# Score products of two heads issued in turn in the short layers of a two-block transformer kernel

## What is computed

```python
def second_block(x, norm_g, w_in, w_out, diff_lam, diff_subln_g, final_norm_g):
    for layer in range(DEPTH):                       # DEPTH = 2
        h = _rmsnorm(x, norm_g[layer])
        proj = jnp.einsum('bsd,de->bse', h, w_in[layer])          # 2048 -> 8 parts of 256
        if layer % 2 == 0:
            oa = _dilated_mixture(_rope(_heads(qa), pos), _rope(_heads(ka), pos), _heads(va))
            ob = _moba(_rope(_heads(qb), pos), _rope(_heads(kb), pos), _heads(vb))
            y = concat(_merge(oa) * silu(ga), _merge(ob) * silu(gb))
        else:
            oc = _diff_attention(...)                # 4 heads, two score maps of 32 features each
            od = _stick_breaking(...)                # 4 heads of 64 features
            y = concat(_merge(oc) * silu(gc), _merge(od) * silu(gd))
        x = x + jnp.einsum('bse,ed->bsd', y, w_out[layer])
    return _rmsnorm(x, final_norm_g)
```

## Time and profile before

| | before |
|---|---|
| executions | 2729.01, 2729.70, 2726.66 us; median 2729.01 |
| profiled execution | span 2726.9 us from its first to its last instruction; no other time is listed for it |
| PE busy | 2696.2 us (99%) |
| DVE busy | 1694.4 us (62%) |
| ACT busy | 1343.5 us (49%) |
| PE waits by the list of waits, whole program | longest kinds 4.8, 4.8, 2.7, 1.4 and 1.3 us |
| layer 4, column slots 812 on | from about 2470 us |
| layer 5, column slots 852 on | from about 2605 us |

### The profile page before, as it was taken

One profiled execution on the slowest core, in us unless ns is written; L12 is line 12 of the kernel. 1 busy time (PEld: TensorE's weight loads), 2 busy tenths in 40 slices (PEclk: granted clock), 3 DMA queues, 4 the chain that ended last, 5 costly groups with the idle time before them and its releaser, 6 DMA issues.

```text
span 2726.9 us, 32209 instructions
## 1 busy us (share of the span) xinstructions
PE 2696.2 (99%) x12944; PEld 2241.6 (82%) x12944; DVE 1694.4 (62%) x2476; ACT 1343.5 (49%) x1952; POOL 63.2 (2%) x85
## 2 busy tenths in 40 slices
PE   9999999999999999999999999999999999999998
PEld 8778888888888888888888888888888888887877
DVE  5677675566666666545645555666666664466666
ACT  6645545464444444434545545644444443355565
POOL 0000000000000000000100000000000000000002
PEclk9999999999999999999999999999999999999999
DMA  7765647656666666656655435566666665565543
GB/s 231 136 139 140 127 122 135 206 186 200 198 194 194 193 193 193 193 193 204 213 172 155 115 110 176 187 193 193 194 193 194 193 195 193 193 202 165 164 137 132
DMA packets 213494, 480.54 MB, mean 176 GB/s; under 512 B 15584, under 2 KB 16480, under 8 KB 212704
## 3 DMA queue, kind: packets, MB, share of 16 engines
q1 hardware_dynamic: 210848, 467.27, 58.9%
q0 software_dynamic: 2352, 11.17, 1.1%
q10 hardware_dynamic: 144, 0.05, 0.0%
HBM read 476.32 MB, written 2.10 MB: 175 GB/s over the span
## 4 chain that ended last, share of the span: by engine, by line
PE 89%; DVE 5%; ACT 3%; issue 1%; DMA 1%; POOL 0%; SPq 0%; ACTq 0%; POOLq 0%
PE PS L1124 19%; PE PS L1126 19%; PE PS L1125 19%; PE PS L1171 8%; PE PS L1173 8%; PE PS L1172 8%; DVE WL L2192 2%; DVE WORK L2359 1%; ACT WH L1664 1%; PE PS L1386 1%; PE PS L1522 1%; PE PS L1099 1%; PE PS L1491 0%; DVE XL L2192 0%; DMA RAW<-in_ffn_w_down 0%
## 5 line engine op out<-in xcount | busy, mean ns | idle before, releaser
L2192 DVE TENSOR_TENSOR WL<-RAW,WH 128x1024 fp32r<-128x1024 f32 x826 | 1011.3, 1226 | 806.1 <-ACT WH L1664 803.6
L1664 ACT ACTIVATE WH<-RAW 128x1024 fp32r<-128x1024 f32 x830 | 875.3, 1056 | 918.8 <-PE PS L1126 609.3
L1124 PE MATMUL PS<-WH,UTH 128*128 128x512 f32 x2396 | 952.4, 397 | 5.0 <-DVE WL L2192 4.8
L1126 PE MATMUL PS<-WH,UTL 128*128 128x512 f32 x2396 | 935.5, 390 | 0.0
L1125 PE MATMUL PS<-WL,UTH 128*128 128x512 f32 x2396 | 934.7, 390 | 0.0
L1124 PEld LDWEIGHTS PS<-WH,UTH 128*128 128x128 f32 x2396 | 450.8, 188 | 102.1 <-DVE WL L2192 5.6
L1126 PEld LDWEIGHTS PS<-WH,UTL 128*128 128x128 f32 x2396 | 450.5, 188 | 96.4
L1125 PEld LDWEIGHTS PS<-WL,UTH 128*128 128x128 f32 x2396 | 451.2, 188 | 88.7
L1171 PE MATMUL PS<-WH,HTH 128*128 128x512 f32 x656 | 255.2, 389 | 0.0
L1172 PE MATMUL PS<-WL,HTH 128*128 128x512 f32 x656 | 255.2, 389 | 0.0
L1173 PE MATMUL PS<-WH,HTL 128*128 128x512 f32 x656 | 255.2, 389 | 0.0
(11 more groups left out here) (426 smaller groups left out, 2176.1 us busy)
## 6 DMA issues: line engine op xcount, KB each, us to landing
RAW<-in_ffn_w_gu SPq DMA_DIRECT2D x352, 512.0 KB, 4.5
RAW<-in_ffn_w_down SPq DMA_DIRECT2D x176, 512.0 KB, 4.4
RAW<-in_ab_w_in SPq DMA_DIRECT2D x128, 512.0 KB, 4.8
RAW<-in_nsa_w_in SPq DMA_DIRECT2D x80, 512.0 KB, 3.7
RAW<-in_w_in SPq DMA_DIRECT2D x64, 512.0 KB, 4.2
RAW<-in_ab_w_out SPq DMA_DIRECT2D x32, 512.0 KB, 4.3
RAW<-in_nsa_w_out SPq DMA_DIRECT2D x32, 512.0 KB, 4.2
RAW<-in_w_out SPq DMA_DIRECT2D x16, 512.0 KB, 4.4
```

The costliest lines, as they stand in the source:

```text
L1124: e.matmul(o, lh, wh[:, j], start=k + j == 0, stop=False)
L1126: x = e.matmul(o, ll, wh[:, j], start=False, stop=k + j == NKT - 1)
L1664: e.activation(wh, raw, ACTF.Copy).then_inc(*a_hi.inc(s))
L2192: e.tensor_tensor(wl, raw, wh.bitcast(F32), ALU.subtract).then_inc(*v_lo.inc(s))
```

## The change

Three steps of PE now make the scores of two heads in one go. They take two banks, and their matmuls alternate between the heads, which lie in different rows of the array: `pl_s(br, i)` for par 0 and 1, `df_s(pair, i)` for heads 2 pair and 2 pair + 1, `st_z(pair)` likewise. The parts that DVE and ACT had under the same names become steps of their own (`pl_x`, `df_x`, `st_x`), one a head: the first head's in the slot of the product, the second's one slot later. What follows (`pl_t`, `df_a`, `st_l`) is now placed from these. No instruction is added or removed on any engine; only order and banks differ.

```diff
+    def plain_scores(br, i):
+        yield from need(("feat", 4, 2 * br))
+        yield from pause(1 + 2 * i)
+        put("pl_s", br, i)
+        put("pl_x", br, 0, i)
+        yield
+        put("pl_x", br, 1, i)
+
     def plain(br, par, i):
-        yield from need(("feat", 4, 2 * br))
-        yield from pause(1 + 2 * par + i)
-        put("pl_s", br, par, i)
-        yield from pause(2)
+        yield from o.behind(2, ("pl_x", br, par, i))
         put("pl_t", br, par, i)
...
+    def diff_scores(pair, i):
+        yield from need(("feat", 5, 0))
+        yield from pause(1 + 4 * pair + 2 * i)
+        put("df_s", pair, i)
+        put("df_x", 2 * pair, i)
+        yield
+        put("df_x", 2 * pair + 1, i)
+
     def diff(h, i):
-        yield from need(("feat", 5, 0))
-        yield from pause(1 + 2 * h)
-        put("df_s", h, i)
-        yield from pause(2)
+        yield from o.behind(2, ("df_x", h, i))
         put("df_a", h, i)
...
+    def stick_scores(pair):
+        yield from need(("feat", 5, 2))
+        yield from pause(1 + 2 * pair)
+        put("st_z", pair)
+        put("st_x", 2 * pair)
+        yield
+        put("st_x", 2 * pair + 1)
+
     def stick(h):
-        yield from need(("feat", 5, 2))
-        yield from pause(1 + h)
-        put("st_z", h)
-        yield from pause(4 - h + h // 2)
+        yield from o.behind(4 - h + h // 2, ("st_x", h))
         put("st_l", h)
...
             @step
-            def pl_s(br, par, i):
-                P, T, s, nk = plain_of(br, par, i)
-                b = take("pl_s", br, par, i)
+            def pl_s(br, i):
+                nk = 128 * (i + 1)
+                b = [take("pl_s", br, par, i) for par in range(2)]
                 on.wait_ge(*a_b2.of("feat", 4, 2 * br, 2))
                 for j in range(2):
-                    q, k = qk_of(4, 2 * br, par + 2 * j)
-                    x = e.matmul(b[:, nk * j:nk * j + nk], q[:, 128 * i:128 * i + 128], k[:, 0:nk], start=True, stop=True)
-                x.then_inc(*p_b2.inc("pl_s", br, par, i))
+                    for par in range(2):
+                        q, k = qk_of(4, 2 * br, par + 2 * j)
+                        x = e.matmul(b[par][:, nk * j:nk * j + nk], q[:, 128 * i:128 * i + 128], k[:, 0:nk],
+                                     start=True, stop=True)
+                        if j == 1:
+                            x.then_inc(*p_b2.inc("pl_s", br, par, i))
```

More of the change, by code:

```diff
@@ L730, in write_order @@
     mixer(4, sink2[4], setup(4, 0, True), setup(4, 2, True),
-          *[plain(br, par, i) for br in range(2) for par in range(2) for i in range(2)],
+          *[plain_scores(br, i) for br in range(2) for i in range(2)],
+          *[plain(br, par, i) for br in range(2) for i in range(2) for par in range(2)],
           *[close(4, 2 * br + 1, *[[("pl_o", br, par, i) for par in range(2)] for i in range(2)])
@@ L738, in write_order @@
     mixer(5, sink2[5], setup(5, 0, True), setup(5, 2, False),
-          *[diff(h, i) for h in range(4) for i in range(2)], *[stick(h) for h in range(4)],
+          *[diff_scores(pair, i) for pair in range(2) for i in range(2)],
+          *[diff(h, i) for h in range(4) for i in range(2)],
+          *[stick_scores(pair) for pair in range(2)], *[stick(h) for h in range(4)],
           close(5, 1), close_diff(), close(5, 3),
@@ L1574, in df_s @@
             @step
-            def df_s(h, i):
-                P, T, s, nk = diff_of(h, i)
-                b = take("df_s", h, i)
+            def df_s(pair, i):
+                nk = 128 * (i + 1)
+                heads = (2 * pair, 2 * pair + 1)
+                b = {h: take("df_s", h, i) for h in heads}
                 on.wait_ge(*a_b2.of("feat", 5, 0, 2))
                 for j in range(2):
-                    q, k = qk_of(5, 0, h, j)
-                    x = e.matmul(b[:, nk * j:nk * j + nk], q[:, 128 * i:128 * i + 128], k[:, 0:nk], start=True, stop=True)
-                x.then_inc(*p_b2.inc("df_s", h, i))
+                    for h in heads:
+                        q, k = qk_of(5, 0, h, j)
+                        x = e.matmul(b[h][:, nk * j:nk * j + nk], q[:, 128 * i:128 * i + 128], k[:, 0:nk],
+                                     start=True, stop=True)
+                        if j == 1:
+                            x.then_inc(*p_b2.inc("df_s", h, i))
             @step
@@ L1604, in st_z @@
             @step
-            def st_z(h):
-                q, k = qk_of(5, 2, h)
-                b = take("st_z", h)
+            def st_z(pair):
+                heads = (2 * pair, 2 * pair + 1)
+                b = {h: take("st_z", h) for h in heads}
+                f = {h: tuple(qk_of(5, 2, h)) for h in heads}
                 on.wait_ge(*a_b2.of("feat", 5, 2, 2))
-                e.matmul(b[:, 0:256], k[:, 0:128], q, start=True, stop=True)
-                x = e.matmul(b[:, 256:384], k[:, 128:256], q[:, 128:256], start=True, stop=True)
-                x.then_inc(*p_b2.inc("st_z", h))
+                for h in heads:
+                    q, k = f[h]
+                    e.matmul(b[h][:, 0:256], k[:, 0:128], q, start=True, stop=True)
+                for h in heads:
+                    q, k = f[h]
+                    x = e.matmul(b[h][:, 256:384], k[:, 128:256], q[:, 128:256], start=True, stop=True)
+                    x.then_inc(*p_b2.inc("st_z", h))
             @step
@@ L2081, in pl_s, with pl_x @@
             @step
-            def pl_s(br, par, i):
+            def pl_x(br, par, i):
                 P, T, s, nk = plain_of(br, par, i)
@@ L2113, in df_s, with df_x @@
             @step
-            def df_s(h, i):
+            def df_x(h, i):
                 P, T, s, nk = diff_of(h, i)
@@ L2140, in st_z, with st_x @@
             @step
-            def st_z(h):
+            def st_x(h):
                 Zs, L = stick_of(h)
```

## The result

The changed kernel took 2738.39 us (median of 5 executions, 2737.49 to 2741.32) against 2728.99 us before (5 executions): 9.4 us longer. The ratio is 1.0038, 95% interval 1.0027 to 1.0049. I had forecast 2735.0, 6.0 us longer. The sign was right; the growth was half as large again as forecast.

What follows compares the result with a forecast made beforehand. PE, 99% busy, was taken as the bound, with the DVE and ACT chain slower where every slot has a link. 0.6 + 3.9 + 1.6 = 6.1 us gave 2735.1, say 2735.0; range 2728 to 2739, leaving out rival 4.

Steps and rivals of the forecast that it cites:

- PE's saving: Score steps of two heads side by side save 8.9 us of PE: layer 4 4.2, df_s 2.6, st_z 2.1.
- The chain: DVE and ACT's links delivering WH and WL, slower than PE's slot: +0.6 us in layer 4, +3.9 in layer 5.
- layer 4 at +0.6: Copies of pl_t now ahead of a prep lengthen the chain by 0.3 us a half; PE's saved 4.2 us return as waits.
- The term of +3.9 us: Layer 5: a link in each slot 856 to 863 delays the last scaling, so slot 868 starts 3.9 us later.
- The clock: One fall of PE's granted clock to 0.50 after the 3.3 us wait before the second st_z: +1.6 us.
- The signs: Wrong if slot 868 comes no later than 2662.80 + 1, layer 4 waits exceed 3 us, or growth lies in layer 4.
- Rival 1: PE waits for the chain but its clock does not fall: +4.5 us, 2733.5; chance 0.27.
- Rival 2: The two heads' products run one after another, mostly hidden by the chain: +1.1 us, 2734.6 to 2736.2; chance 0.13.
- Rival 3: PE's lead entering layer 5 covers the chain, last wait about 1 us without a fall: about 0, 2729; chance 0.12.
- Rival 4: Saved PE time reaches the end, if links cost under about 3.2 us: -8.9 us, 2720.1, half realised 2724.5; chance 0.08.

Runs made afterwards that it cites:

- even_later: Changed kernel with both softmaxes of a pair in their product's slot, and st_l, st_m, st_a, st_w in their slots from before; 2719.7 us, ratio 0.9968.
- changed_again: The changed kernel run once more without alteration, with a second profile; 2736.2 us, ratio 1.0032.
- serial: The changed kernel with the products of its joint steps issued one head after the other, not in turn; 2738.9 us, ratio 1.0035.
- keep_busy: The changed kernel with 8 to 13 products of zeros ahead of the four places where PE waited 1.8 to 2.9 us; 2733.3 us, ratio 1.0017.
- rhythm_only: The changed kernel with products again one head at a time, each in the slot of its softmax; softmaxes stay in the changed slots; 2731.1 us, ratio 1.0010.
- layer4_only: Layer 4 as in the changed kernel, layer 5 as before; 2732.5 us, ratio 1.0012.
- busy_single_z: As keep_busy, but st_z products one head at a time and the zeros for slot 863 moved to slot 864; 2736.6 us, ratio 1.0033.

## Why the prediction was right or wrong

**PE's saving: right.** 8.9 us of PE time, of which row groups running side by side was the unproven part. The records show it: eight in 0.72 us. In even_later, where nothing stands against it, the two layers are 4.5 + 3.6 = 8.1 us shorter. It is the Trainium skill's rule that small matmuls in different row groups run at once ("TensorE: Matmul & The Clock Gate", "Part 3: Packing small matmuls — row/col tiling"), and the traces now agree with it for row groups too.

**The chain: right, to a few tenths.** I had priced layer 4 at +0.6; with the clock held it was +0.7 (no run here separates its two halves). I had added up 33.0 us from the first to the last scaling of layer 5. The changed kernel's first is the mark at 2625.99; its seventh and last (timeline of DVE):

```profile
2652.76 0.69 DVE L2755 SCALAR_TENSOR_TENSOR WORK<-PS,BIG 128x512 f32<-128x512 f32 x1 [0.25 <-PE PS L1604]
2658.86 0.68 DVE L2755 SCALAR_TENSOR_TENSOR BIG<-PS,BIG 128x512 f32<-128x512 f32 x1
```

2658.86 - 2625.99 = 32.9. The last link, with passes of `st_z` in it, is 6.1 us, where 4.74 and the 1.15 and 0.3 that I had put there make 6.2. The term of +3.9 us measured +3.7 with the clock held. Together the chain costs 4.4 us where I had 4.5.

**The clock: the step that failed.** The prediction says "I add one fall, +1.6 us" and "A fall after an earlier wait costs nothing, since PE then meets the chain again." The first is wrong in number. I priced only the wait of 3.3 us, although show a stretch at 0.50 behind a wait of 2.36, and although I had myself forecast four more waits of about 2 us. The two profiles of the changed kernel have six and three stretches. The second sentence is wrong wherever the chain starts from PE again. In layer 4 the next meeting place lies behind `feat` and the score products of the second half, which PE itself must make first, so a stretch behind slot 822 is paid nearly in full (+2.2 or +2.3 instead of +0.7, for 1.7 us of lost work); the wait in slot 829 is 2.0 us with that stretch (changed_again) and without it (serial). In layer 5 it depends: in changed_again a stretch from 2646.4 on made the products of slot 862 late, and the scaling behind them waited for PE (timeline of DVE in changed_again):

```profile
2652.82 0.69 DVE L2755 SCALAR_TENSOR_TENSOR WORK<-PS,BIG 128x512 f32<-128x512 f32 x1 [1.54 <-PE PS L1604]
```

In the changed kernel's first profile, with its stretch at 2642, that wait was 0.25 us, and the stretch was mostly hidden by a shorter wait at the next bank, 0.6 us in slot 861 where changed_again waited 2.1. The term of +1.6 us measured 9.4 - 5.0 = 4.4 us in the medians (keep_busy's 2733.3 is 5.0 over its own before), 8.2 - 5.0 = 3.2 with changed_again, and 12.0 - 4.4 = 7.6 in the first profile. With 4.4 instead of 1.6 the sum would have been 2737.9.

**The signs.** Of the three by which I would be wrong, the one on layer 4's growth came partly true: layer 4 has 5.4 of the 12.0 us of growth in the two layers in the first profile and 2.3 of 9.1 in changed_again. It was the clock and not the chain, which has 0.7 of 4.4 there. Another came true if its 3 us are meant for all waits of layer 4 together (4.3 us by those over half a us), and not if they are meant for one (2.0). Slot 868 starts at 2675.20, and counted from the first scaling (2625.99, and 2620.01 before) that is 6.4 us later than before, against the 6 forecast with a stretch; in keep_busy (2668.01, from 2621.74) it is 3.5, against 3.9.

**The rivals.** Rival 1 (waits, no fall) is keep_busy: 2733.5 forecast, 2733.3 measured. Rival 2 fell, since side by side is what happens, and even without issuing in turn. Rival 3 fell: there was no slack. Rival 4's number came true in another arrangement, even_later at 2719.7, though not by the condition that was named for it (links under about 3.2 us): there two softmaxes share a slot (scalings at 2614.27 and 2615.06), the next slot is free for DVE and ACT to catch up, and the first to the last scaling of layer 5 is 24.5 us instead of 32.9.

The Trainium skill's caution that tiling speeds up TensorE but not the emptying of PSUM ("TensorEngine Tiling (Array Packing)", "PSUM Bottleneck") held for this placement and not for the idea: with the softmaxes bunched the same emptying kept up.

**Not settled.** What decides whether a wait of about 2 us is followed by none, one or two stretches; and the 0.9 us between rhythm_only and keep_busy in layer 5.

## What to carry to other kernels

Time saved on the busiest engine arrives only if its suppliers have a free slot to catch up; keep the bunching of side work when you merge steps, and check every step that counts its slot from the one you moved. When a change creates waits of some 2 us on TensorE (here from 1.6 us on), price each of them with the clock behind it, and ask whether the next meeting point starts from TensorE's own work, because then the loss isn't hidden. If a wait can't be removed, products of zeros that fit into it cost nothing that showed here and held the clock.

## What the hardware showed that I had not expected

- Products of two row groups run side by side when they merely stand next to each other: eight records in 0.72 us with one head's four ahead of the other's, the same as in turn.
- Waits of 1.8 to 2.3 us of TensorE had 3.41 or 6.83 us at granted clock 0.50 at their end in some executions and none in others, with the same wait to 0.1 us; the wait of 2.9 us had one or the other in all four profiles that have it (the 2.0 us wait of slot 829: 6.82 us in one profile, 3.41 in `serial`, none in layer4_only and changed_again).
- Multiplying 128x128 zeros kept the granted clock at 1.00 through such waits: all four places in keep_busy, three in busy_single_z, whose fourth wait (4.3 us, without zeros) had 6.83 us at 0.50.
